# First quarter of the output projection moved among the last two tasks of mixer C, values ahead of the turn in C, first and last rows of work re-dealt

## The reference, cut to what matters

```
proj = x @ w_in                                   # 1024 x 2578
A: differential attention, 6 heads   -> 384       # "tasks" 0 to 17 of the kernel
B: causal pooling mixer              -> 256
C: attention with compressed, selected and window keys, 6 heads -> 384   # tasks 18 to 32
mix = concat(A, B, C) @ w_out                     # the output projection, 1024 x 1024
x = layer_norm(ALPHA * x + mix)
x = layer_norm(ALPHA * x + relu(x @ w_up)**2 @ w_down)
```

## Time and profile before

| | |
|---|---|
| median of three runs | 1260.44 us (1260.19 to 1260.78) |
| profiled execution, its own time | 1260.26 us |
| its span in the trace | 1258.4 us |
| PE busy | 1237.9 us (98%), 7118 matmuls |
| PEld busy | 1028.7 us (82%) |
| DVE busy | 725.6 us (58%) |
| ACT busy | 477.6 us (38%) |
| POOL busy | 493.0 us (39%) |
| PE's share of the chain that ended last | 91% |
| granted TensorE clock, mean | 0.998 |

### The profile page before, as it was taken

How to read it: one execution, slowest core, us unless ns; L and a number is a source line. 1 busy time by engine, 2 the same in 40 slices (tenths; PEclk the granted TensorE clock), 3 DMA queues, 4 the chain that set the end, 5 groups by cost and what they waited for, 6 DMA issues and landing times.

```text
span 1258.4 us, 17853 instructions
## 1 busy us (share of the span) xinstructions
PE 1237.9 (98%) x7118; PEld 1028.7 (82%) x7118; DVE 725.6 (58%) x1117; ACT 477.6 (38%) x946; POOL 493.0 (39%) x279
## 2 busy tenths in 40 slices
PE   7999999999999999999999999999999999999997
PEld 7998766789888888888899976668988888888885
DVE  4395778369672262360397868783796623605406
ACT  5226688523232221222143366784333322222210
POOL 3468000134544444444345760003264444444442
PEclk9999999999999999999999999999999999999999
DMA  7433001123523332233224320013233332332211
GB/s 252 124 80 102 2 18 35 67 84 102 162 94 101 101 99 88 98 101 96 63 60 128 93 68 1 18 52 100 69 129 105 101 100 89 97 101 101 96 55 67
DMA packets 77826, 110.04 MB, mean 87 GB/s; under 512 B 17648, under 2 KB 38448, under 8 KB 77616
## 3 DMA queue, kind: packets, MB, share of 16 engines
q1 hardware_dynamic: 76160, 104.11, 27.4%
q10 hardware_dynamic: 1584, 4.78, 1.2%
HBM read 106.78 MB, written 2.10 MB: 87 GB/s over the span
## 4 chain that ended last, share of the span: by engine, by line
PE 91%; DVE 4%; issue 1%; ACT 1%; POOL 1%; DMA 0%; DVEq 0%; POOLq 0%; ACTq 0%
PE ps L678 16%; PE ps L679 16%; PE ps L680 16%; PE ps L675 9%; PE ps L674 9%; PE ps L676 9%; PE ps L781 3%; PE ps L769 3%; PE ps L818 2%; PE ps L803 1%; PE ps L633 1%; DVE negmax L1390 1%; ACT probs_a L1134 1%; PE ps L894 1%; PE ps L856 1%
## 5 line engine op out<-in xcount | busy, mean ns | idle before, releaser
L542 POOL TENSOR_TENSOR w_lo<-raw,w_hi 128x1024 fp32r<-128x1024 f32 (+3 forms) x184 | 425.0, 2314 | 644.7 <-ACT w_hi L1006 644.2
L1006 ACT ACTIVATE w_hi<-raw 128x1024 fp32r<-128x1024 f32 (+3 forms) x200 | 199.0, 996 | 598.2 <-PE ps L680 365.7
L674 PE MATMUL ps<-xt_hi,w_lo 128*128 128x512 f32 (+1 forms) x576 | 210.7, 366 | 0.0
L675 PE MATMUL ps<-xt_hi,w_hi 128*128 128x512 f32 (+1 forms) x576 | 210.5, 365 | 0.0
L676 PE MATMUL ps<-xt_lo,w_hi 128*128 128x512 f32 (+1 forms) x576 | 210.5, 365 | 0.0
L678 PE MATMUL ps<-w_hi,xt_lo 128*128 128x384 f32 (+3 forms) x448 | 152.0, 339 | 1.6 <-DVE xt_lo L1242 1.1
L678 PE MATMUL ps<-w_hi,mt_lo 128*128 128x512 f32 x384 | 150.1, 391 | 0.0
L679 PE MATMUL ps<-w_hi,mt_hi 128*128 128x512 f32 x384 | 149.4, 389 | 0.0
L680 PE MATMUL ps<-w_lo,mt_hi 128*128 128x512 f32 x384 | 149.4, 389 | 0.0
L680 PE MATMUL ps<-w_lo,xt_hi 128*128 128x384 f32 (+3 forms) x448 | 147.5, 329 | 0.0
L679 PE MATMUL ps<-w_hi,xt_hi 128*128 128x384 f32 (+3 forms) x448 | 147.4, 329 | 0.0
(11 more groups left out here) (175 smaller groups left out, 1875.1 us busy)
## 6 DMA issues: line engine op xcount, KB each, us to landing
raw<-in_w_up SPq DMA_DIRECT2D x64, 512.0 KB, 3.7
raw<-in_w_down SPq DMA_DIRECT2D x64, 512.0 KB, 3.9
raw<-in_w_in SPq DMA_DIRECT2D x32, 384.0 KB, 3.3
raw<-in_w_in SPq DMA_DIRECT2D x16, 256.0 KB, 2.8
raw<-in_w_in SPq DMA_DIRECT2D x32, 128.0 KB, 2.9
raw<-in_w_out SPq DMA_DIRECT2D x8, 512.0 KB, 3.4
raw<-in_w_out SPq DMA_DIRECT2D x12, 256.0 KB, 3.7
rows<-in_ln_g ACTq DMA_DIRECT2D x4, 512.0 KB, 4.3
```

The lines of the kernel that those rows point to most:

```text
L542: nc.gpsimd.tensor_tensor(unit_of(w_lo, u), unit_of(raw, u), unit_of(w_hi, u).bitcast(F32), ALU.subtract).then_inc(s_lo_ready, 1)
L674: mm(o, wl[:, c], a_hi[:, k, cols], start=first, stop=False)
L675: mm(o, wh[:, c], a_hi[:, k, cols], start=False, stop=False)
L1006: A(unit_of(w_hi, u), unit_of(raw, u), ACT.Copy).then_inc(s_hi_ready, 1)
```

## The change

Five edits. (1) PE order in C: for t from 19 to 32 `values(t - 1)` comes ahead of `turn_p(t)`. (2) The 24 matmuls of unit 0 of the output projection are dealt out: at t = 31 k = 0 and 1 for banks 2 and 3, at t = 32 k = 0 and 1 for banks 0 and 1, each ahead of the values; after task 32 come unit 1, `values(32)`, units 2 and 3. (3) In ACT's order the rounding of a unit at t = 19, 25, 27, 28 comes behind `copy_p(t - 1)`. (4) Head: the low parts of units 0 and 1 of layer 0 are made by DVE, unit 0 ahead of the first tile of x, unit 1 between tiles 1 and 2. (5) Tail: tile 2 is scaled ahead of tile 3, tile 3 in two halves of 512 columns, each stored by its own DMA.

```
@@ -517,10 +517,14 @@
                         sp.wait_ge(s_x_normed, nth("x_normed", layer, TT))
                         parameters(layer + 1, 4 * (u - U_MLP - 12), 4 * (u - U_MLP - 11))
                     unit(layer, u)
-            for n, tt in enumerate((0, 1, 3, 2)):
-                sp.wait_ge(s_out_last, n + 1)
+            for tt in range(3):
+                sp.wait_ge(s_out_last, tt + 1)
                 sp.dma_start(out[0, tt * P:(tt + 1) * P, :], xres[:, tt]).then_inc(s_stored, 16)
-            sp.wait_ge(s_stored, 16 * TT)
+            for half in range(2):
+                sp.wait_ge(s_out_last, 4 + half)
+                c = slice(512 * half, 512 * half + 512)
+                sp.dma_start(out[0, 3 * P:4 * P, c], xres[:, 3, c]).then_inc(s_stored, 16)
+            sp.wait_ge(s_stored, 16 * (TT + 1))
 
 
         @block.gpsimd
@@ -569,8 +573,6 @@
 
             nc.gpsimd.memset(w_blk[:], 0.0).then_inc(s_blk_zero, 1)
             for layer in range(DEPTH):
-                if layer == 0:
-                    split(layer, 0, 2)
                 split(layer, 4, U_LAST - 2)
                 pool.wait_ge(s_const_in, 32)
 
@@ -956,6 +958,18 @@
                     elif k >= M_C:
                         pe.wait_ge(s_oc_mixed, nth("oc_mixed", layer, k - M_C + 1))
 
+                def first_of_out(layer, t):
+
+                    pe.wait_ge(s_exped, nth("exped", layer, t + 1))
+                    pe.wait_ge(s_lo_ready, nth("lo_ready", layer, U_OUT + 1))
+                    pe.wait_ge(s_hi_ready, nth("hi_ready", layer, U_OUT + 1))
+                    for k in range(2):
+                        mixed(k)
+                        for b in (2 * (t % 2), 2 * (t % 2) + 1):
+                            last = products(IN_CHUNKS, k, b, 0, mt_hi, mt_lo)
+                    if t == TASKS - 1:
+                        last.then_inc(s_unit_used, 1)
+
                 for t in range(TASKS):
                     if t < 2 * BOTH - 2 and t % 2:
                         scores_of_both(layer, t + 1)
@@ -963,16 +977,21 @@
                         last_chunk(layer, n)
                     if 2 * BOTH - 2 <= t < TASKS - 2:
                         scores(layer, t + 2)
-                    if turns(t):
+                    if t >= TASKS - 2:
+                        first_of_out(layer, t)
+                    if t > TASKS_A:
+                        values(layer, t - 1)
                         turn_p(layer, t)
-                    if t >= 1 and turns(t - 1):
-                        values(layer, t - 1)
+                    else:
+                        if turns(t):
+                            turn_p(layer, t)
+                        if t >= 1 and turns(t - 1):
+                            values(layer, t - 1)
                     if t in SIDE:
                         side(layer, t)
-                pe.wait_ge(s_exped, nth("exped", layer, TASKS))
-                gemm(layer, IN_CHUNKS, 0, mt_hi, mt_lo, mixed, (0,))
+                gemm(layer, IN_CHUNKS, 0, mt_hi, mt_lo, mixed, (1,))
                 values(layer, TASKS - 1)
-                gemm(layer, IN_CHUNKS, 0, mt_hi, mt_lo, mixed, (1, 2, 3))
+                gemm(layer, IN_CHUNKS, 0, mt_hi, mt_lo, mixed, (2, 3))
                 gemm(layer, IN_CHUNKS + 1, 4, mt_hi, mt_lo, mixed, by_bank=2, ahead=lambda: turn_half(layer, 1, 0))
 
                 for k in range(N_MLP):
@@ -1160,14 +1179,14 @@
                 for t in range(TASKS):
                     if t >= 2:
                         exps(t)
-                    if t in OUT_SPLIT:
-                        split_to(layer, U_OUT + OUT_SPLIT.index(t) + 1)
                     if t == 10:
                         act.wait_ge(s_cmp_shifted, nth("cmp_shifted", layer, 1))
                         by_tile = cmp_s.rearrange("p i s n -> p i (s n)")
                         A(by_tile, by_tile, ACT.Exp).then_inc(s_cmp_exp, 1)
                     if t and turns(t - 1):
                         copy_p(t - 1)
+                    if t in OUT_SPLIT:
+                        split_to(layer, U_OUT + OUT_SPLIT.index(t) + 1)
                     if t in LAST_COPIED:
                         b = LAST_COPIED[t]
                         if b < 3:
@@ -1245,7 +1264,8 @@
             def low_unit(layer, u):
 
                 g = layer * UNITS + u
-                dve.wait_ge(s_lo_ready, nth("lo_ready", layer, u))
+                if g:
+                    dve.wait_ge(s_lo_ready, nth("lo_ready", layer, u))
                 dve.wait_ge(s_hi_ready, nth("hi_ready", layer, u + 1))
                 if g >= RING:
                     dve.wait_ge(s_unit_used, g - RING + 1)
@@ -1287,20 +1307,23 @@
                     link(V.bn_aggr(mv[:, tt, :], bst[:, tt].rearrange("p a s -> p (a s)")))
                     V.tensor_scalar(mv[:, tt, 1:2], mv[:, tt, 1:2], LN_EPS, None, ALU.add).then_inc(s_stats, 1)
 
-                def scale_and_shift(tt):
+                def scale_and_shift(tt, parts=1):
                     dve.wait_ge(s_rstd, nth("rstd", layer, TT + tt + 1))
                     dve.wait_ge(s_out_centred, tt + 1)
-                    V.scalar_tensor_tensor(xres[:, tt], xres[:, tt], rstd[:, tt:tt + 1], rows[:, 1], ALU.mult, ALU.add) \
-                        .then_inc(s_out_last, 1)
+                    n = D // parts
+                    for c in range(0, D, n):
+                        xs = xres[:, tt, c:c + n]
+                        V.scalar_tensor_tensor(xs, xs, rstd[:, tt:tt + 1], rows[:, 1, c:c + n], ALU.mult, ALU.add).then_inc(s_out_last, 1)
 
                 if final:
                     for tt in range(TT):
                         sums_of(tt)
                         V.scalar_tensor_tensor(xres[:, tt], xres[:, tt], mv[:, tt, 0:1], rows[:, 0], ALU.subtract, ALU.mult) \
                             .then_inc(s_out_centred, 1)
-                        if tt in (0, 1, 3):
+                        if tt < 2:
                             scale_and_shift(tt)
                     scale_and_shift(2)
+                    scale_and_shift(3, 2)
                 else:
                     then = (layer + 1, 0) if ln else (layer, 1)
                     u = 0 if ln else U_MLP
@@ -1326,7 +1349,10 @@
             V.memset(lnp[:, 3, :], 0.0).then_inc(s_ones, 1)
             for layer in range(DEPTH):
                 if layer == 0:
-                    split_x(layer, 0, 0, range(5))
+                    low_unit(layer, 0)
+                    split_x(layer, 0, 0, (0, 1))
+                    low_unit(layer, 1)
+                    split_x(layer, 0, 0, (2, 3, 4))
                     low_unit(layer, 2)
                     split_x(layer, 0, 0, (5,))
                     low_unit(layer, 3)
```

10 lines of the change are left out of this document (6 added, 4 removed).

## The result

| | before | after |
|---|---|---|
| median of 22 runs each | 1260.37 us (1260.13 to 1260.78) | 1262.22 us (1261.65 to 1262.89) |
| profiled execution, its span | 1260.26, 1258.4 | 1261.81, 1260.0 |
| start of the last matmul | 1248.67 | 1250.74 |
| ratio of the medians | | 1.0015, 95% interval 1.0009 to 1.0021 |

The kernel is 1.85 us slower: 0.15%, within the predicted range of 1261.4 to 1267.0 and on the predicted side, but half of the 3.7 us forecast, and under the 0.2% that the prediction set as its bound. The case that happened is "no change that can be told" by that bound, which had 0.25.

What follows compares the result with a forecast made beforehand. PE, busy throughout at full clock, was taken as the bound. Per layer -0.78 + 0.42 + 1.0 + 2.15 = +2.8, twice +5.6; with -1.25 and -0.65, +3.7: 1264.0 us, range 1261.4 to 1267.0.

Steps and rivals of the forecast that it cites:

- no change that can be told: Outcome for the whole kernel: within some 0.2%, 2.5 us, of before; chance 0.25.
- Term 1: End of mixer C: 12 matmuls ahead of turns 31 and 32 close PE's gaps; -0.78 us a layer.
- Term 2: Output projection's blocks: four entries instead of two, at 0.21 us; +0.42 us a layer, bounds 0 and 0.8.
- Term 3: Mixer C, values ahead of turn: PE's scores wait for ACT's round; +1.0 us a layer, bounds 0 and 2.2.
- Term 4: Behind values(32): k = 4 waits 1.50 us for its chain, k = 5 another 0.65; +2.15 us a layer.
- Term 5: Head: without POOL, PE's 1.1 us wait goes and the first product starts earlier; -1.25 us, bounds 0.3 and 1.8.
- Term 6: Tail: DVE's idle time filled, 0.35 us, and a smaller last store, 0.3; -0.65 us in all.
- (b): Mixer C: ACT's round fits, so no stall at the scores; 1262.0 us, chance 0.22.
- (c): Mixer C: copy does not arrive under the scores, twelve tasks wait some 0.1 us more; 1266.6 us, chance 0.18.
- (d): Behind values(32): k = 4 does not wait, so the change wins; 1257.7 us, chance 0.05.

Runs made afterwards that it cites:

- version with turn first: Changed kernel with turn ahead of values in C and rounding ahead of the copy, as before; filling, head and tail kept: 1262.42 us, ratio 1.0015.
- the order alone: Kernel before with only values ahead of the turn in C and the rounding behind the copy: 1263.63 us, one run.
- version with both mends: Changed kernel with values(32) between the halves of unit 1 and the roundings at tasks 19 to 22: 1254.59 us, ratio 0.9957.
- the tail's experiment: Kernel before with only the new tail (tile 2 scaled first, tile 3 in halves with a store each): 1259.91 us, ratio 0.9996.
- the roundings early: Changed kernel with the four roundings at tasks 19 to 22 instead of 19, 25, 27, 28: 1259.78 us, ratio 0.9995.

## Why the prediction was right and wrong

The forecast of +2.8 us a layer came out as +1.70, measured; the -1.9 for head and tail as -1.8, both in the profiled execution. That the time fell within the range is in part luck. A gain of 1.3 us a layer stood in no term; stalls 0.65 larger than forecast hid half of it. With the stalls at the size forecast the sum would have been 1260.9, under the range, as an estimate from these terms.

**Term 1, gaps filled, -0.78: right.** After, no turn waits for DVE; in the version with turn first the waits are gone as well, so it is the blocks that close the gaps, as said.

**Term 2, more switches, +0.42: did not happen.** I priced an entry from the block of unit 0, which is left and entered through a values step. A block between turn and values costs 0.85 + 2.92 us (228.41 to 229.26 to 232.18) against 1.02 + 2.72 for the parts: 0.03 each. Three of them in place of one entry at 0.21 are worth -0.1. I gave 0 as the lower bound and took 0.42. It is the new order that makes them cheap: in the version with turn first the three cost 0.43, and there about half of the term is real.

**Term 3, ACT's round, +1.0: right in kind, too small, and not the whole of the order's effect.** Start to start the waits are 0.34 at scores(28) (0.15 forecast), 0.72 at scores(30) (0.52) and 0.35 at scores(31) (0.25); the one of 0.1 at t = 23 did not come, and one of 0.24 at `values(18)` came that I had not worked out: its first matmuls write bank 7, which ACT's copy and squares of mixer A's last pair must have read (L1202, L1203, at 178.19 to 179.27), and these stand behind the copy and a rounding in ACT's order while the values now come a turn earlier. Together +1.65. The step that failed is the first of this part: I took the turn at 1.02 wherever it stands. Behind it now come masks or side work instead of values, and it takes 0.93: 0.09 less at eleven turns, and three side steps that follow a turn take 0.87 (185.60 to 186.47) instead of 0.97 (186.85 to 187.82 before). That is -1.3 us a layer, which no term had. With -0.78, -0.1 and +1.65 it makes -0.5; measured is -0.59 (66.05 against 66.64), so some 0.1 is left unexplained. The rows for it stood in the trace before, where the last turn ahead of mixer C has side work behind it (timeline of PE, before):

```profile
173.28 1.09 PE L781 MATMUL ps<-kc,probs_a 128*128 128x128 f32 x8
174.21 0.60 PE L881 MATMUL ps<-kc,proj_b 128*128 128x128 f32 x4
```

That is 0.93, against 1.02 in the earlier trace rows. The experiments bear out both the cost and the gain: without the roundings' stalls the interval falls by 1.42, and from there, without the order, it rises by 1.53.

**Term 4, behind values(32), +2.15: right.** It measured +2.28: k = 4 late by 1.58 (1.50 forecast), k = 5 by 0.56 (0.65), and the rest in entries. The chain is the one forecast, ACT at +0.11, DVE at +0.74, PE at +1.58 after the values step ends:

```profile
240.83 0.60 ACT L1166 ACTIVATE mt_hi<-ps 128x512 fp32r<-128x512 f32 x1 [2.67 <-PE ps L820]
...
241.46 0.69 DVE L1476 TENSOR_TENSOR mt_lo<-ps,mt_hi 128x512 fp32r<-128x512 f32 x1 [13.07 <-ACT mt_hi L1166]
```

Parting unit 1 took back 2.3 us a layer. The second chunk did not wait for POOL, as said.

**Term 5, the head, -1.25: right in the trace (-1.32), not in every run.** DVE does the instructions at the times forecast, here the first three (timeline of DVE after):

```profile
7.36 0.96 DVE L1272 TENSOR_TENSOR w_lo<-raw,w_hi 128x768 fp32r<-128x768 f32 x1 [6.34 <-ACT w_hi L1025]
8.24 0.29 DVE L1260 CAST xt_hi<-tmp 128x256 fp32r<-128x256 f32 x1
8.56 0.42 DVE L1261 TENSOR_TENSOR xt_lo<-tmp,xt_hi 128x256 fp32r<-128x256 f32 x1
```

With POOL out, the cast takes 0.29. Beside POOL it took 1.28 and ended 0.14 us behind POOL's subtraction. The Trainium skill (SBUF — State Buffer, SBUF: two separate sides) says that an operation of DVE and one of GpSimd that want the port pair they share do not share its bandwidth but take turns by whole instructions; the trace agrees, within the roughness of POOL's spans, by that 0.14. The sum under the term was misread all the same: the wait of 1.1 that was to go has 0.3 in it that lies at the start of layer 1 and stayed. The head's 0.80 of idle time cost more than its figure, 1.13 us from the sixth product to the seventh (10.88 to 12.01), where the kernel after has 0.18 (10.60 to 10.78). This 0.95, the first product 0.30 earlier (9.63 against 9.93) and some 0.1 in the steps make the 1.32; that 1.1 and 0.15 came near it is luck. What I left out is that the first 1 to 2 us of PE's products vary from run to run, shown below.

**Term 6, the tail, -0.65: mis-sized.** The scaling gave 0.40, where 0.35 was said; the smaller last store, forecast at 0.3, gave less than 0.1 (0.44 in all at the median of eleven runs). The Trainium skill (DMA: Bandwidth & Descriptors, Anatomy of one DMA) has a part that grows with the bytes, for the other kind of queue; the estimate from it is that the half store lands 0.6 sooner. Here 256 KB and 512 KB both took 2.7 us, so no such part shows between these sizes.

**The rivals.** (b), no stall in ACT's round, came nearest in time (1262.0) and was wrong in kind: the stalls are there, and a gain that nobody had listed hides them. (c), the copy not under the scores, did not happen in the twelve tasks; the 0.1 us of margin held, though it fails at once where no scores cover it (1.11 us in the order alone). (d), the change wins if the 1.5 us behind `values(32)` were hidden, was right as a condition: with unit 1 parted the kernel took 1257.85 against the 1257.7 worked out for it, though with other terms under that sum (stalls in ACT's round, and the cheaper steps). In the chances, 0.70 for slower by over 0.2% rested on the term of the order being a pure loss, between 0 and 2.2; the gain in it that was not seen is what moved the time under the bound.

## What to carry to other kernels

When a reordering is costed, the price of a step belongs to the pair: read the start-to-start time of each step in every place where it stands, by what is ahead of it and what follows it, before taking one figure for it. Before work is moved forward as a filler, ask what it was hiding where it stood: here 5.5 us of matmuls covered a three-engine chain, and leaving half of them in place took back 4.4 us at the medians. And the spare work of an engine that works in order belongs ahead of its wait: here the rounding ahead of the copy saved 0.73 us a layer, in one run.

## What the runs showed of the hardware

**The price of a step goes by its neighbours.** Eight transposes take 1.02 us from start to start with values behind them, 0.93 with bf16 masks or side products, 0.85 with a float32r block of 512 columns, in all tasks of layer 0 without a wait, and the same in those of layer 1 (803.55 to 804.48). What stands ahead counts too: a side step of two products takes 0.97 behind values and 0.87 behind a turn, and a turn ahead of values takes 0.97 behind a block (227.86 to 228.83, version with turn first) instead of 1.02. What in the engine makes it so was not tried.

**The first products run at either pace.** With the new head, `scores(20)` came at 173.56 to 173.64 us in four profiled executions and at 174.23 to 175.65 in four others; with the old head at 174.88 to 175.18 in all four. The timeline of PE in the head of the version with both mends, which had the latest:

```profile
7.07 3.89 PE L635 MATMUL ps<-kc,xres 128*128 128x128 f32 x16 [7.07 <-DMA xres<-in_x]
10.61 0.67 PE L680 MATMUL ps<-w_hi,xt_lo 128*128 128x384 f32 x1
11.07 0.52 PE L681 MATMUL ps<-w_hi,xt_hi 128*128 128x384 f32 x1
11.39 0.52 PE L682 MATMUL ps<-w_lo,xt_hi 128*128 128x384 f32 x1
...
12.98 0.34 PE L681 MATMUL ps<-w_hi,xt_hi 128*128 128x384 f32 x1
13.15 0.34 PE L682 MATMUL ps<-w_lo,xt_hi 128*128 128x384 f32 x1
```

and of the kernel after:

```profile
6.38 3.49 PE L635 MATMUL ps<-kc,xres 128*128 128x128 f32 x16 [6.38 <-DMA xres<-in_x]
9.63 0.42 PE L680 MATMUL ps<-w_hi,xt_lo 128*128 128x384 f32 x1
9.89 0.33 PE L681 MATMUL ps<-w_hi,xt_hi 128*128 128x384 f32 x1
10.06 0.34 PE L682 MATMUL ps<-w_lo,xt_hi 128*128 128x384 f32 x1
```

Of the 2.0 us, 0.7 are a later x (7.07 against 6.38), and about 1.3 a slower pace: the first product comes 3.54 us behind x instead of 3.25, and products step by 0.32 us until 12.67, where the kernel after steps by 0.17 or 0.18. Ahead of both PE had done only the same 16 transposes since the launch. The window 10 to 13 us shows a granted clock of 1.00 all the same (stretch, length, busy per engine, PEclk, DMA):

```profile
10.00:13.00 3.00, 3.00 (x13) 3.00 (x12) 2.71 (x8) 3.00 (x6) 0.00 (x0) 1.00 1.06 411
```

so at the start of an execution the pace has to be read from the steps. The ratio of the paces would fit the lower of the clock's two levels, 1.2 GHz for 2.4, but no row shows it. The old head is deaf to this: in the tail's experiment the first five products step by 0.47 to 0.28 too, but the seventh had to wait for DVE's subtraction, which ended at 12.19 there and at 11.96 before, and came at 12.24, beside 12.01 before. Taking that wait away gained 1.2 us at the median of the best version and exposed a scatter that it had covered. Both parts can be told apart in the eight profiled executions. From x to `scores(20)` 167.25 to 167.44 us pass in the four at the full pace, and 167.64, 167.99, 168.14 and 168.58 in the others, which have one, three, three and five steps of 0.32 and one or two in between. The pace alone is enough: with the roundings early x came at 6.44, only 0.06 later than after, and `scores(20)` 0.94 later. What sets the pace stays open, and neither part was controlled in any run or is recorded in the runs without a profile.
